# Seven block products per pair of residues for two value projections, and squares ordered ahead of copies in the attention

## Chip, cores and metric

One core of one Trainium2 chip runs one program with one launch. The metric is the device time in microseconds (us) from start to end of an execution. The page's names: PE is TensorE's matmuls, PEld its weight loads, DVE is VectorE, ACT ScalarE, POOL GpSimd, SP SyncE.

## What is computed

The program computes several transformer-like blocks for 512 tokens of width 1024, in float32. The change is in the first block, in its attention. With `h = rms_norm(x)`, the projection `proj = h @ w_in` gives queries, keys and values for three groups of eight heads of width 64:

```
qkv_a = qkv_a.reshape(b, s, 3, N_ATTN_GROUPS, HEADS_PER_GROUP, HEAD_DIM_A)
qa = rms_norm(qkv_a[:, :, 0], q_norm[i])
ka = rms_norm(qkv_a[:, :, 1], k_norm[i])
va = qkv_a[:, :, 2]
for gi, (win, dil) in enumerate(((128, 1), (512, 4), (2048, 16))):
    o_g, lse_g = dilated_window_attention(qa[:, :, gi], ka[:, :, gi], va[:, :, gi], win, dil)
mix_w = jax.nn.softmax(jnp.stack(lses, axis=0), axis=0)
```

Group 0 attends within a window of 128 tokens; groups 1 and 2 attend with a step of 4 and 16. So the kernel keeps the values of group 0 by blocks of 128 consecutive tokens, and those of the groups 1 and 2 by residue: block b holds the tokens b, b + 4, b + 8, ...

## The kernel before

Five engines run one hand-written order each, and meet at semaphores. All weights come in one stream of 1 MB fills through `ring`, four slots in SBUF. SP requests fill n + 4 once `slot_free` says that the first matmul of fill n + 1 is done (line 4348). The activations lie transposed in `hT`: eight chunks of 128 features (partitions) by 512 tokens.

**Values (lines 800 to 828).** `values_pe` goes over three groups, eight chunks k and four blocks b. The stationary operand is a block of tokens of `hT`, the moving one 512 columns of weights. For group 0 a block is 128 tokens side by side; for groups 1 and 2 it is `ap[:, b::4]`, every fourth token (`tokens_of`, line 797). The groups take two fills each, and PSUM banks 0 to 3, 4 to 7, 0 to 3. `values_dve` first makes four differences of quarters of `hT` into `in_sums` (lines 814 to 820), which the attention's projections need, then copies each group's four banks to `va` (line 824). ScalarE and POOL have nothing to do with the values, but for POOL's sums on the weights of the first projection fill (`slot_sums_pool`, lines 740 to 748).

**Projections in the attention (lines 702 to 796).** Queries and keys come from 12 fills of 28 matmuls each: seven block products instead of eight, for two tiles of 128 features and two halves of the tokens. The products' sums of weights are made by POOL in place, those of the activations are `in_sums`. The parts land in the two banks of `acc` (6 and 7). ScalarE copies the first two (`parts_out_act`, line 757, after product 1) and the third product's (`swap_out_act`, line 762, after product 3) to `kept`; VectorE joins the rest (`left_dve`, `right_dve`, `last_dve`). The last join ends with a tick (line 1051) that raises `qk_out`. Product 4 of a fill waits for the first copy, product 6 for the second.

**The loop of units (lines 934 to 955, 1012 to 1030, 1118 to 1138).** The attention proper has 32 units n: scores, maxima, exponentials, a transposition of the probabilities, the product with the values. In a unit, TensorE runs `turn_probs(n)`, `scores(n + 2)`, two to four products of the projection fills (`qk_parts`, by a fixed table of steps), then `head_sums(f)` for a fill f that became complete, and `mix_values(n)`. `head_sums` waits for the squares of that fill. ScalarE runs in a unit `turned(n)` (line 997), the first copy of the fill in work (and its second copy, if the same unit holds that), then `square(f)` of the fill that became complete (lines 968 and 970), else the second copy, `exps(n + 2)` (line 988), and `root(f)` (lines 976 and 979: logarithm and exponential, each with its table load):

```
turned(n)
for f in fills_of_step(n, "two"):
    parts_out_act(e, f)
    if f in fills_of_step(n, "left"):
        swap_out_act(e, f)
for f in done:
    square(f)
```

A fill completes in one unit and the next fill's first two products fall into the next, so the squares of the one and the copies of the other stand in the same unit (n = 0, 3, 6, 8, 11, 14, 16, 19, 22). In n = 6, 14 and 22 both copies stand there.

Later stages wait on counts of the same semaphores (`seven`, `seven_read`, `w_sum`, `base_in`, `h_sum`).

## Time and profile before

| | |
|---|---|
| median of 3 runs | 2614.75 us (2613.24 to 2618.49) |
| the profiled execution | 2618.45 us |
| its span, first to last instruction | 2616.0 us |
| TensorE's mean granted clock | 0.992 |
| TensorE matmuls busy | 2539.7 us (97%) |
| VectorE, ScalarE, POOL busy | 1303.1, 640.2, 329.5 us |
| moved by DMA | 227.41 MB, mean 87 GB/s |

A profile is one execution. Its page gives busy time by engine, the chain of work that ended last and the costliest groups; the trace behind it answers by stretch, by line and by wait. A float32 matmul stands there as two records, and so does its weight load. "Idle before" a group is the time that its engine had nothing in work, with what ended it. All of TensorE's products of this kernel have line 404, the helper that issues them, and are told apart by operands and time. The values are the stretch from 20.2 to 102.7 us, the attention follows until about 357 us.

### The profile page before, as it was taken

The page shows a single profiled execution, that of the slowest core. Times are in us where ns is not written, and L with a number is a line of the kernel's source. Part 1 is how long each engine was busy: PE and PEld are TensorE (multiplying, and loading weights), DVE is VectorE, ACT ScalarE, POOL GpSimd, SP SyncE. Part 2 cuts the span into 40 slices and gives each one's busy share as a digit, 9 for nine tenths or more (in the row PEclk, how much of TensorE's full clock was granted, in tenths as well). Part 3 has the DMA queues.
Part 4 walks back from the last instruction along what each step waited for, and adds up shares of the span by engine and source line. Part 5 has one row for each costly group of instructions (what it writes and reads, how often), then busy time and mean ns, then how long its engine had stood idle before and what let it go on. Part 6 is the DMA issues. An engine that isn't in the chain of part 4 may idle for free.

```text
span 2616.0 us, 38542 instructions
## 1 busy us (share of the span) xinstructions
PE 2539.7 (97%) x15741; PEld 1748.8 (67%) x15741; DVE 1303.1 (50%) x2873; ACT 640.2 (24%) x1168; POOL 329.5 (13%) x315
## 2 busy tenths in 40 slices
PE   8999998999999999999999999999999999999998
PEld 4766756777775684444444446688864575888887
DVE  2244565757632251000035845676765675777733
ACT  1156643323430222110011144212110122121201
POOL 0222115445441400000001000000000000000000
PEclk9999999999999999999999999999999999999999
DMA  4211111111113232444413110222223212222222
GB/s 188 77 63 49 49 56 58 39 45 52 49 50 138 88 109 81 167 171 161 174 67 113 65 48 33 89 81 97 81 97 112 97 35 81 84 94 81 95 83 80
DMA packets 32520, 227.41 MB, mean 87 GB/s; under 512 B 3552, under 2 KB 4192, under 8 KB 6112
## 3 DMA queue, kind: packets, MB, share of 16 engines
q1 hardware_dynamic: 30384, 219.50, 23.5%
q10 hardware_dynamic: 1968, 5.51, 0.6%
q8 instruction: 125, 2.05, 0.3%
q14 instruction: 43, 0.35, 0.0%
HBM read 222.90 MB, written 2.10 MB: 86 GB/s over the span
## 4 chain that ended last, share of the span: by engine, by line
PE 90%; DVE 4%; ACT 3%; issue 2%; POOL 1%; DMA 0%; ACTq 0%; DVEq 0%; POOLq 0%
PE psum L404 88%; PE psum L907 1%; DVE work L1613 0%; ACT work L970 0%; PE psum L2977 0%; PE psum L2638 0%; ACT work L3031 0%; PE psum L1262 0%; ACT work L968 0%; ACT work L976 0%; ACT L976 0%; ACT work L988 0%; DVE work L1920 0%; POOL ring L1455 0%; POOL ring L1438 0%
## 5 line engine op out<-in xcount | busy, mean ns | idle before, releaser
L404 PE MATMUL psum<-hT,ring 128*128 128x256 f32 (+2 forms) x2872 | 542.8, 370 | 4.0 <-issue 1.7
L404 PEld LDWEIGHTS psum<-hT,ring 128*128 128x128 f32 (+1 forms) x2872 | 371.9, 161 | 135.7 <-issue 94.0
L404 PE MATMUL psum<-work,ring 128*128 128x256 f32 (+1 forms) x1176 | 378.0, 472 | 4.6 <-ACT work L3903 2.4
L404 PEld LDWEIGHTS psum<-work,ring 128*128 128x128 f32 x1176 | 222.0, 190 | 144.3 <-issue 121.6
L404 PE MATMUL psum<-xT,ring 128*128 128x256 f32 (+2 forms) x1184 | 293.1, 400 | 15.6 <-POOL ring L1438 7.1
L404 PE MATMUL psum<-work,mixT 128*128 128x256 f32 (+2 forms) x1332 | 289.3, 379 | 1.2 <-DVE mixT L4118 0.7
L404 PEld LDWEIGHTS psum<-work,mixT 128*128 128x128 f32 (+1 forms) x1332 | 232.1, 182 | 47.7 <-issue 16.3
L404 PE MATMUL psum<-work 32*32 32x32 f32 (+8 forms) x5374 | 255.5, 248 | 8.4 <-issue 3.7
L404 PEld LDWEIGHTS psum<-work 32*32 32x32 f32 (+5 forms) x5374 | 210.5, 124 | 78.0 <-issue 51.9
L404 PEld LDWEIGHTS psum<-xT,ring 128*128 128x128 f32 (+1 forms) x1184 | 211.0, 188 | 71.2 <-issue 25.7
L404 PE MATMUL psum<-ring,work 128*128 (+1 forms) x568 | 247.0, 593 | 0.6 <-DVE work L3198 0.6
L404 PEld LDWEIGHTS psum<-ring,work 128*128 128x128 f32 x568 | 106.7, 190 | 131.1 <-issue 127.9
L3502 DVE SCALAR_TENSOR_TENSOR work<-work,vec 128x512 f32<-128x512 f32 x176 | 125.6, 748 | 67.3 <-ACT work L3441 67.3
L3420 POOL TENSOR_TENSOR ring<-ring,vec 128x1024 f32<-128x1024 f32 x6 | 11.3, 1898 | 1098.0 <-DMA ring<-stream_dram 1098.0
L404 PE MATMUL psum<-mixT,ring 128*128 128x512 f32 x320 | 146.7, 604 | 1.9 <-ACT mixT L3057 1.4
L3491 DVE TENSOR_TENSOR work<-work,psum 128x256 f32<-128x256 f32 x294 | 115.8, 417 | 64.2 <-PE psum L404 62.6
L404 PE MATMUL psum<-ring,hT 128*128 128x512 f32 (+1 forms) x304 | 131.7, 592 | 1.0 <-DVE ticks L379 1.0
L404 PEld LDWEIGHTS psum<-ring,hT 128*128 128x128 f32 x304 | 72.5, 240 | 56.7 <-issue 39.9
L2732 DVE SCALAR_TENSOR_TENSOR work<-psum,work 128x256 f32<-128x256 f32 x28 | 13.0, 482 | 194.3 <-ACT work L2714 193.8
L404 PEld LDWEIGHTS psum<-mixT,ring 128*128 128x128 f32 x320 | 61.0, 194 | 69.1 <-issue 64.7
L3434 ACT ACTIVATE work<-psum 128x256 f32<-128x256 f32 x42 | 16.1, 384 | 323.4 <-PE psum L404 323.4
L547 ACT ACTIVATE work<-xT 128x512 f32<-128x512 f32 x56 | 34.7, 628 | 224.6 <-DVE xT L2163 185.4
(498 smaller groups left out, 2757.1 us busy)
## 6 DMA issues: line engine op xcount, KB each, us to landing
ring<-stream_dram SPq DMA_DIRECT2D x204, 1024.0 KB, 4.8
con<-consts_dram SPq DMA_DIRECT2D x1, 2953.0 KB, 13.5
mixT<-x_dram ACTq DMA_DIRECT2D x4, 512.0 KB, 6.6
work<-x_dram ACTq DMA_DIRECT2D x4, 512.0 KB, 6.3
out_dram<-mixT SPq DMA_DIRECT2D x4, 512.0 KB, 3.6
work<-p_dram ACTq DMA_DIRECT2D x1, 512.0 KB, 6.0
con<-ssm_dram ACTq DMA_DIRECT2D x1, 512.0 KB, 3.6
vec<-vecs_dram SPq DMA_DIRECT2D x1, 378.0 KB, 5.9
```

The source lines that it names most:

```text
L404: ins = self.eng.matmul(out, lhsT, rhs, start=start, stop=stop)
L547: nc.scalar.activation(squares[:, k, :], xT[:, k, :], ACT.Square).then_inc(S["x_squares"], 1)
L907: ins = e.eng.transpose(psum[:, 2, at:at + P], a_pr[:, u.d, at:at + P], ident)
L2732: nc.vector.scalar_tensor_tensor(out=act_tok[:, s, :], in0=psum[:, gate_up_bank(ex, s), 256:512], scalar=slot_weight[:, ex, s:s + 1], in1= ...
L3420: ins = nc.gpsimd.tensor_tensor(w, w, bc(V(gain), P), ALU.mult)
L3434: nc.scalar.activation(base[:, j % 2, :], seven(j, 0), ACT.Copy).then_inc(S["base_in"], 1)
L3491: nc.vector.tensor_tensor(o, in0, in1, ALU.add).then_inc(S["seven_read"], 1)
L3502: nc.vector.scalar_tensor_tensor(out=y, in0=fpad[:, half, t - 1:t - 1 + T], scalar=wv[:, t - 1:t], in1=y, op0=ALU.mult, op1=ALU.add).then_ ...
```

## The change

For the groups 1 and 2 the blocks are taken in pairs: two residues (0 and 1, then 2 and 3) by two halves of the 1024 features, times two halves of the features by two halves of the 512 columns, with seven products of 128 tokens by 256 columns over four chunks each, in place of eight. Four such pairs (two groups, two pairs of residues) are numbered j = 0 to 3. VectorE first makes four differences of `hT` by residue (`residue_sums`, into `mixT`), then four sums on the weights of a group's two fills in eight steps (`value_weights_dve`, one of them in place in `ring`), then the four old differences, the copies of group 0, join 0, the weights of group 2, joins 1 to 3. ScalarE copies one bank for each pair (`values_act`). Group 0 is as before. The two fills of a group are both held until both pairs have used them: the second slot is given free at product 4 of the second pair. TensorE's wait ahead of the attention is now for the joins of the first three pairs.

In the attention `square(f)` of the done fills stands directly behind `turned(n)`, ahead of the copies of the next fill.

Elsewhere in the kernel the counts waited for grow by the four products' sets (`PAIRED` = 4 and `IN_SUMS` = 8 in place of 0 and 4), with no other change.

```
                 if i == 1:
                     if f == 0:
-                        e.eng.wait_ge(S["h_sum"], 4)
+                        e.eng.wait_ge(S["h_sum"], IN_SUMS)
...
+        residue_sums = mixT[:, 4:12, :].rearrange("p a t -> p (a t)").rearrange("p (n k c t) -> p n k c t", n=4, k=4, c=2)
+        value_sums = work[:, GROUPS * NB * 512:GROUPS * NB * 512 + 12 * T].rearrange("p (g n k t) -> p g n k t", g=2, n=3, k=4)
+        value_base, value_two = kept[:, T:T + T // 2], kept[:, T + T // 2:2 * T]
+        PAIRED, RESIDUE_SUMS, IN_SUMS = 4, {"one": 1, "three": 2, "two": 3, "four": 4}, 8
+        VALUE_SUMS = {"one": 2, "three": 4, "two": 6, "four": 8}
+        def value_part(j, i):
+            n, at = ((0, 0), (0, 1), (1, 0), (2, 0), (2, 1), (1, 1), (3, 0))[i]
+            return psum[:, 4 - 4 * (j % 2) + n, T // 2 * at:T // 2 * at + T // 2]
         def values_pe(e):
-            for g in range(GROUPS):
-                for k in range(DC):
-                    if k % 4 == 0:
-                        e.eng.wait_ge(S[e.landing()], e.landed())
-                        w = e.slot(ring)
-                    for b in range(NB):
-                        if g == 2 and k == 0 and b == 0:
-                            e.eng.wait_ge(S["values_out"], 1)
-                        ins = e.mm(psum[:, 4 * (g % 2) + b, :], tokens_of(g, b, hT[:, k, :]), w[:, 512 * (k % 4):512 * (k % 4) + 512],
-                                   k == 0, k == DC - 1)
-                ins.then_inc(S["values"], 1)
+            for k in range(DC):
+                if k % 4 == 0:
+                    e.eng.wait_ge(S[e.landing()], e.landed())
+                    w = e.slot(ring)
+                for b in range(NB):
+                    ins = e.mm(psum[:, b, :], tokens_of(0, b, hT[:, k, :]), w[:, 512 * (k % 4):512 * (k % 4) + 512],
+                               k == 0, k == DC - 1)
+            ins.then_inc(S["values"], 1)
+            fill_at["values"] = e.c["fill"].n
+            for j in range(PAIRED):
+                g, pair = divmod(j, 2)
+                f = fill_at["values"] + 2 * g
+                if pair == 0:
+                    e.eng.wait_ge(S[e.landing()], e.landed())
+                    low = e.slot(ring)
+                high = ring[:, (f + 1) % RING, :]
+                def block(w, half):
+                    return [w[:, 512 * k + 256 * half:512 * k + 256 * half + 256] for k in range(4)]
+                def tokens(k0, r):
+                    return [hT[:, k0 + k, 2 * pair + r::4] for k in range(4)]
+                def product(i, tok, weights):
+                    for k in range(4):
+                        ins = e.mm(value_part(j, i), tok[k], weights[k], k == 0 and i in (0, 2, 3, 6), k == 3 and i in (1, 4, 5, 6))
+                    ins.then_inc(S["seven"], 1)
+                t1, t2, t3, t4 = ([residue_sums[:, n, k, pair, :] for k in range(4)] for n in range(4))
+                s1, s2, s4 = ([value_sums[:, g, n, k, :] for k in range(4)] for n in range(3))
+                if j == 1:
+                    e.eng.wait_ge(S["values_out"], 1)
+                if j >= 2:
+                    e.eng.wait_ge(S["base_in"], j - 1)
+                product(0, tokens(0, 0), block(low, 0))
+                e.eng.wait_ge(S["w_sum"], 8 * g + VALUE_SUMS["one"])
+                e.eng.wait_ge(S["h_sum"], RESIDUE_SUMS["one"])
+                product(1, t1, s1)
+                e.eng.wait_ge(S["loaded%d" % ((f + 1) % RING)], 16 * ((f + 1) // RING + 1))
+                if j >= 2:
+                    e.eng.wait_ge(S["seven_read"], 7 * (j - 1))
+                product(2, tokens(4, 0), block(high, 0))
+                e.eng.wait_ge(S["w_sum"], 8 * g + VALUE_SUMS["three"])
+                e.eng.wait_ge(S["h_sum"], RESIDUE_SUMS["three"])
+                product(3, t3, block(low, 1))
+                if pair == 1:
+                    e.slot(ring)
+                e.eng.wait_ge(S["w_sum"], 8 * g + VALUE_SUMS["two"])
+                e.eng.wait_ge(S["h_sum"], RESIDUE_SUMS["two"])
+                product(4, t2, s2)
+                e.eng.wait_ge(S["w_sum"], 8 * g + VALUE_SUMS["four"])
+                product(5, tokens(4, 1), s4)
+                e.eng.wait_ge(S["h_sum"], RESIDUE_SUMS["four"])
+                product(6, t4, block(high, 1))
+            e.c["fast"].n += PAIRED
+        def values_act(e):
+            for j in range(PAIRED):
+                e.eng.wait_ge(S["seven"], 7 * j + 2)
+                if j >= 1:
+                    e.eng.wait_ge(S["seven_read"], 7 * (j - 1) + 6)
+                nc.scalar.activation(kept[:, 0:T], psum[:, 4 - 4 * (j % 2), :], ACT.Copy).then_inc(S["base_in"], 1)
+            e.c["fast"].n += PAIRED
+        def value_weights_dve(e, g):
+            f = fill_at["values"] + 2 * g
+            (a11, a21), (a12, a22) = ([ring[:, n % RING, :].rearrange("p (k h t) -> p h k t", k=4, h=2)[:, h, :, :] for h in range(2)]
+                                      for n in (f, f + 1))
+            s1, s2, s4 = (value_sums[:, g, n, :, :] for n in range(3))
+            for n in (f, f + 1):
+                e.eng.wait_ge(S["loaded%d" % (n % RING)], 16 * (n // RING + 1))
+            for step, (o, in0, in1, op) in enumerate(((s1, a21, a22, ALU.add), (a21, a11, a21, ALU.subtract),
+                                                      (s2, s1, a11, ALU.subtract), (s4, a12, s2, ALU.subtract))):
+                if step:
+                    e.eng.wait_ge(S["w_sum"], 8 * g + 2 * (1, 1, 3)[step - 1])
+                for k in (slice(0, 2), slice(2, 4)):
+                    nc.vector.tensor_tensor(o[:, k, :], in0[:, k, :], in1[:, k, :], op).then_inc(S["w_sum"], 1)
+        def value_joins_dve(e, j):
+            g, pair = divmod(j, 2)
+            read = S["seven_read"]
+            x, y = va[:, 1 + g, 2 * pair, :], va[:, 1 + g, 2 * pair + 1, :]
+            first, second = slice(0, 256), slice(256, 512)
+            zero, one = kept[:, 0:T // 2], kept[:, T // 2:T]
+            e.eng.wait_ge(S["base_in"], j + 1)
+            e.eng.wait_ge(S["seven"], 7 * j + 5)
+            nc.vector.tensor_tensor(value_base, zero, value_part(j, 4), ALU.add).then_inc(read, 1)
+            e.eng.wait_ge(read, 7 * j + 1)
+            nc.vector.tensor_tensor(value_two, value_base, value_part(j, 3), ALU.add).then_inc(read, 1)
+            e.eng.wait_ge(read, 7 * j + 2)
+            nc.vector.tensor_tensor(y[:, second], value_two, one, ALU.add).then_inc(read, 1)
+            e.eng.wait_ge(read, 7 * j + 3)
+            nc.vector.tensor_tensor(one, value_base, one, ALU.add).then_inc(read, 1)
+            e.eng.wait_ge(S["seven"], 7 * j + 6)
+            nc.vector.tensor_tensor(x[:, first], zero, value_part(j, 2), ALU.add).then_inc(read, 1)
+            e.eng.wait_ge(read, 7 * j + 4)
+            nc.vector.tensor_tensor(y[:, first], one, value_part(j, 5), ALU.add).then_inc(read, 1)
+            e.eng.wait_ge(S["seven"], 7 * j + 7)
+            nc.vector.tensor_tensor(x[:, second], value_two, value_part(j, 6), ALU.add).then_inc(read, 1)
 
         def values_dve(e):
+            low, high = (hT[:, k, :].rearrange("p k (m r) -> p k r m", r=NB) for k in (slice(0, 4), slice(4, 8)))
+            xs, ys_ = slice(0, 4, 2), slice(1, 4, 2)
+            for n, (o, in0, in1) in enumerate(((0, low[:, :, ys_, :], low[:, :, xs, :]), (2, high[:, :, ys_, :], low[:, :, ys_, :]),
+                                               (1, high[:, :, ys_, :], residue_sums[:, 0, :, :, :]),
+                                               (3, high[:, :, xs, :], residue_sums[:, 1, :, :, :]))):
+                if n >= 2:
+                    e.eng.wait_ge(S["h_sum"], (1, 3)[n - 2])
+                nc.vector.tensor_tensor(residue_sums[:, o, :, :, :], in0, in1, ALU.subtract).then_inc(S["h_sum"], 1)
+            value_weights_dve(e, 0)
             k1, k2, early, late = slice(0, 4), slice(4, 8), slice(0, T // 2), slice(T // 2, T)
             for n, (o, in0, in1) in enumerate(((0, hT[:, k1, late], hT[:, k1, early]), (2, hT[:, k2, late], hT[:, k1, late]),
                                                (1, hT[:, k2, late], in_sums[:, 0, :, :]),
                                                (3, hT[:, k2, early], in_sums[:, 1, :, :]))):
                 if n >= 2:
-                    e.eng.wait_ge(S["h_sum"], (1, 3)[n - 2])
+                    e.eng.wait_ge(S["h_sum"], RESIDUE_SUMS["four"] + (1, 3)[n - 2])
                 nc.vector.tensor_tensor(in_sums[:, o, :, :], in0, in1, ALU.subtract).then_inc(S["h_sum"], 1)
-            for g in range(GROUPS):
-                e.eng.wait_ge(S["values"], e.c["values"].next())
-                for b in range(NB):
-                    ins = nc.vector.tensor_copy(va[:, g, b, :], psum[:, 4 * (g % 2) + b, :])
-                    if b < NB - 1:
-                        ins.then_inc(S["dve_chain"], 1)
-                        e.eng.wait_ge(S["dve_chain"], e.c["dve_chain"].next())
-                ins.then_inc(S["values_out"], 1)
+            e.eng.wait_ge(S["values"], e.c["values"].next())
+            for b in range(NB):
+                ins = nc.vector.tensor_copy(va[:, 0, b, :], psum[:, b, :])
+                if b < NB - 1:
+                    ins.then_inc(S["dve_chain"], 1)
+                    e.eng.wait_ge(S["dve_chain"], e.c["dve_chain"].next())
+            ins.then_inc(S["values_out"], 1)
+            value_joins_dve(e, 0)
+            value_weights_dve(e, 1)
+            for j in range(1, PAIRED):
+                value_joins_dve(e, j)
+            e.c["fast"].n += PAIRED
 
...
             for n in range(UNITS_A):
                 done = [AHEAD // 2 - 1] if n == 0 else fills_of_step(n - 1, "last")
                 turned(n)
+                for f in done:
+                    square(f)
                 for f in fills_of_step(n, "two"):
                     parts_out_act(e, f)
                     if f in fills_of_step(n, "left"):
                         swap_out_act(e, f)
-                for f in done:
-                    square(f)
                 for f in fills_of_step(n, "left"):
                     if f not in fills_of_step(n, "two"):
                         swap_out_act(e, f)
...
             e.c["stage"].next()
-            e.eng.wait_ge(S["values_out"], 2)
+            e.eng.wait_ge(S["seven_read"], 7 * (PAIRED - 1))
             e.mark("attn")
...
             e.eng.wait_ge(S["stage"], e.c["stage"].next())
             e.mark("values")
+            values_act(e)
             e.eng.wait_ge(S["stage"], e.c["stage"].next())
```

## Rows read from the trace of the kernel before

**Rows 1.** Parts 1 and 4 of the page: busy time, and the chain that ended last

```profile
PE 2539.7 (97%) x15741; PEld 1748.8 (67%) x15741; DVE 1303.1 (50%) x2873; ACT 640.2 (24%) x1168; POOL 329.5 (13%) x315
...
PE 90%; DVE 4%; ACT 3%; issue 2%; POOL 1%; DMA 0%; ACTq 0%; DVEq 0%; POOLq 0%
```

**Rows 2.** Busy us (instructions) of PE, PEld, DVE, ACT, POOL; clock; DMA: values, attention

```profile
20.20:102.70 82.50, 82.47 (x192) 51.73 (x193) 10.25 (x12) 0.00 (x0) 2.53 (x2) 1.00 0.28 106
102.70:330.00 227.30, 211.09 (x1190) 160.23 (x1189) 109.74 (x406) 122.50 (x231) 58.22 (x46) 0.98 0.16 56
```

**Rows 3.** Waits of TensorE, 99 to 350 us: total us, times, longest

```profile
PE psum L404 <- ACT work L970: 11.5, 9, 2.3
```

**Rows 4.** Busy time as in rows 2, within group 0 and within group 1

```profile
20.30:47.20 26.90, 26.90 (x63) 12.00 (x64) 4.63 (x4) 0.00 (x0) 0.00 (x0) 1.00 0.40 161
...
58.00:85.50 27.50, 27.50 (x65) 19.74 (x64) 2.76 (x4) 0.00 (x0) 2.53 (x2) 1.00 0.21 76
```

**Rows 5.** Timeline of TensorE's weight loads, attention: start us, us taken

```profile
107.70 3.43 PEld L404 LDWEIGHTS psum<-xT,ring 128*128 128x128 f32 x16
```

**Rows 6.** Timeline of TensorE's weight loads under single-column matmuls, near 972 us

```profile
971.70 1.86 PEld L404 LDWEIGHTS psum<-con,work 128*128 128x128 f32 x16 [0.20 <-DVE work L555]
```

**Rows 7.** Page part 6; groups by line, 0 to 200 us; timelines of VectorE and SP

```profile
con<-consts_dram SPq DMA_DIRECT2D x1, 2953.0 KB, 13.5
...
L820 DVE TENSOR_TENSOR xT<-hT 128x1024 f32<-128x1024 f32 x2 | 2.4, 1221 | 0.0
...
11.26 1.23 SPq L610 DMA_DIRECT2D ring<-stream_dram  x2
...
113.63 0.41 DVE L777 TENSOR_TENSOR work<-mixT,psum 128x256 f32<-128x256 f32 x1
...
126.94 0.60 DVE L777 TENSOR_TENSOR work<-mixT,psum 128x256 f32<-128x256 f32 x1
```

**Rows 8.** Timeline of the unit n = 3 and the next, 168 to 183 us

```profile
168.80 0.06 DVE L1051 MEMSET ticks<- 128x1 f32 x1
...
168.91 0.60 ACT L997 ACTIVATE work<-psum 128x512 f32<-128x512 f32 x1 [2.69 <-PE psum L907]
...
173.21 0.60 ACT L757 ACTIVATE mixT<-psum 128x512 f32<-128x512 f32 x1 [3.70 <-PE psum L404]
...
174.35 1.27 ACT L970 ACTIVATE work<-work 64x512 f32<-64x512 f32 x2
...
175.67 1.09 PE L404 MATMUL psum<-work,con 64*64 64x512 f32 x8 [0.77 <-ACT work L970]
...
176.75 1.28 ACT L976 ACT_TABLE_LOAD   x1
...
181.43 0.58 ACT L997 ACTIVATE work<-psum 128x512 f32<-128x512 f32 x1
...
182.15 0.66 PE L404 MATMUL psum<-work 128*64 128x128 f32 x8
```

**Rows 9.** Timeline of the unit n = 6, 189 to 199 us

```profile
189.90 0.06 DVE L1051 MEMSET ticks<- 128x1 f32 x1 [0.50 <-DVE work L791]
...
192.98 0.60 ACT L757 ACTIVATE mixT<-psum 128x512 f32<-128x512 f32 x1 [3.48 <-PE psum L404]
...
198.68 1.09 PE L404 MATMUL psum<-work,con 64*64 64x512 f32 x8 [2.28 <-ACT work L970]
```

**Rows 10.** As rows 2, clock 0.50; timeline of TensorE, n = 6, n = 14

```profile
200.20:203.40 3.20, 3.20 (x14) 1.93 (x11) 0.96 (x6) 3.16 (x4) 0.00 (x0) 0.50 0.02 5
...
199.70 0.77 PE L404 MATMUL psum<-work 128*64 128x128 f32 x8
...
202.60 2.43 PE L404 MATMUL psum<-xT,ring 128*128 128x256 f32 x8
...
260.17 0.66 PE L404 MATMUL psum<-work 128*64 128x128 f32 x8
...
261.98 1.99 PE L404 MATMUL psum<-xT,ring 128*128 128x256 f32 x8
```

More of the change, by code:

```diff
@@ L2130, in out_weights_dve @@
             if n >= 2:
-                e.eng.wait_ge(S["seven"], 7 * (n - 2) + 6)
+                e.eng.wait_ge(S["seven"], 7 * (PAIRED + n - 2) + 6)
             nc.vector.tensor_tensor(s1, a21, a22, ALU.add).then_inc(S["w_sum"], 1)
-            e.eng.wait_ge(S["w_sum"], 4 * n + 1)
+            e.eng.wait_ge(S["w_sum"], 4 * (PAIRED + n) + 1)
             nc.vector.tensor_tensor(a21, a11, a21, ALU.subtract).then_inc(S["w_sum"], 1)
             nc.vector.tensor_tensor(s2, s1, a11, ALU.subtract).then_inc(S["w_sum"], 1)
-            e.eng.wait_ge(S["w_sum"], 4 * n + 3)
+            e.eng.wait_ge(S["w_sum"], 4 * (PAIRED + n) + 3)
             nc.vector.tensor_tensor(s4, a12, s2, ALU.subtract).then_inc(S["w_sum"], 1)
@@ L2211, in x_added @@
         def x_added(c):
-            return 7 * (c // 2) + 6 + c % 2
+            return 7 * (PAIRED + c // 2) + 6 + c % 2
         def x_turn_chunk_pe(e, c):
@@ L2301, in out_kept_act @@
         def out_kept_act(e, n):
-            e.eng.wait_ge(S["seven"], 7 * n + 2)
+            e.eng.wait_ge(S["seven"], 7 * (PAIRED + n) + 2)
             if n == 0:
@@ L3269, in program @@
                      work[:, FC * T:FC * T + 4 * T]]
-        DOWN_AT, G_AT = 2 * FAST + NB, 12
+        DOWN_AT, G_AT = 2 * FAST + NB + PAIRED, IN_SUMS + 8
         def group(q, i):
```

40 lines of the change are left out of this document (20 added, 20 removed).

## The prediction

> **What bounds the kernel now.** I read the page first [rows 1]: TensorE is busy 97% of the span and carries 90% of the chain that ended last, while VectorE has 4% and ScalarE 3% of it. DMA is nowhere on the chain. So a microsecond taken from TensorE's queue early on is a microsecond of the end, unless another engine becomes late. The table by stage [rows 2] then gives the two stages that are edited: the values (20.2 to 102.7 us) have TensorE busy without a hole, 82.47 of 82.50 us in 192 records, and only 10.25 us of VectorE and none of ScalarE; the attention (102.7 to 330 us) has 16.2 us in which TensorE is not busy. The waits of TensorE in the attention [rows 3] name the largest part of these holes: 11.5 us in nine places until the squares of line 970 are done, at most 2.3 us at a time. The profiled execution took 2618.45 us (span 2616.0); the median of the three runs is 2614.75, 3.7 us less. I make the sum of differences against the profiled one and apply it to the median, which I forecast. No change means within 0.2%, 5.2 us.
>
> **Part 1, the values of two groups.** Removed: 2 x 8 x 4 = 64 products of 512 columns. In the trace each product is two matmul records (96 products, 192 records [rows 2]), 0.430 us each, so the 64 cost 128 x 0.430 = 55.0 us. Added: 4 pairs x 7 products x 4 chunks = 112 products of 256 columns, 224 records. The attention's products have this form. Sixteen of its weight loads, one to a matmul record, take 3.43 us, the last of them 0.19 [rows 5]: one starts every (3.43 - 0.19) / 15 = 0.216 us. At that price the new work is 224 x 0.216 = 48.3 us, a gain of 6.7.
>
> That price holds for weights that lie side by side. Products 0, 2 and 5 take the tokens straight from hT with a step of four (12 of the 28 in each pair, 96 records), the other four from the packed differences. The kernel before loads with that step in its groups 1 and 2: a load there takes 19.74 us / 64 = 0.308 us, in group 0, without the step, 12.00 / 64 = 0.19 us [rows 4]. Under 0.43 us of matmul the longer load is hidden; under 0.216 us it isn't, if it counts in full. What it counts is bounded so. Below: all hidden, gain 6.7 us. Above: loads follow one another as those of rows 5 do, 0.19 us plus a gap of 0.025; the stepped ones would come each 0.333 us, 96 x 0.117 = 11.2 us dearer, a loss of 4.5. The nearest row says which: under matmuls of a single column, sixteen loads of 0.19 us take 1.86 us [rows 6], so one starts each (1.86 - 0.19) / 15 = 0.111 us: 0.08 us of a load's record overlaps the next load. So I take 0.308 - 0.08 = 0.228 us for a stepped one, 0.012 over the matmul, 96 x 0.012 = 1.2 us. **Part 1: -5.5 us.**
>
> The Trainium skill (SBUF — State Buffer, "Door 1: The DMA port swizzle") has a rule that speaks against this: lines of 16 bytes, each access that crosses into a new one paying a penalty. By it every token of these loads pays, as the 0.308 against 0.19 us bears out; it has no figure for a load, and so moves nothing in the sum.
>
> What stands beside: TensorE's first 32 products stay (27.5 us, until 47.7). VectorE in that time makes four subtractions of 1024 elements with a step. Without one they took 1.22 us [rows 7]; a stepped operand took 0.60 where 256 elements otherwise took 0.42 [rows 7], so up to 2 us each, 8 in all. Then the weights' sums, 8 x 512 elements, 0.7 us each (half of 1.22, rounded up), 5.6 us, behind the landing of the third and fourth slot, issued at 11.3 to 12.5 us [rows 7]; at the 13.5 us of the slowest issue on the page that is 26 us. Then the four old subtractions, 4.9 us. End near 26 + 5.6 + 4.9 = 37 to 40 us, 8 us before the copies of group 0. I cost all this at nothing; were the cover gone, product 1 at 49.6 us would wait. The joins: ScalarE copies one bank (0.6 us), VectorE adds seven times 256 elements, 7 x 0.42 to 0.60 = 3 to 4 us for 12.2 us of TensorE. The second weights' sums (5.6 us) stand behind join 0 (near 61 us) and are wanted near 74. Behind the last product one addition of 0.42 us is left, and TensorE goes on anyway, since it waits for join 2 alone; ScalarE is wanted first at the end of the attention's second product, 16 x 0.216 = 3.5 us in. SP's fills: the first attention fill is now requested at product 4 of the second pair, near 67 us, and used near 97, with two sums of POOL between; even 13.5 us of transfer leave room. The third is requested at product 4 of the last pair, near 92, and used 24 us later. Nothing waits.
>
> **Part 2, squares first.** In nine of the units of the loop (n = 0, 3, 6, 8, 11, 14, 16, 19, 22) ScalarE squares a finished fill and copies the next one's parts in one unit. Rows 8 show one: turned(3) is done at 169.5, the fill's tick came at 168.80, and ScalarE is then idle 3.70 us until product 1 of the next fill has ended; only behind that copy come the squares, the last of them until 175.62. TensorE has ended its third product at 174.90 and waits 0.77 us with the head sums. With the squares first they run 169.5 to 171.4, 1.8 us before the copy can start; exps(n+2) behind them come 1.9 us earlier. Six units are like this, 6 x 0.77 = 4.6 us. In n = 6, 14, 22 both copies come first, and the wait is 2.28 us [rows 9]: 6.8 us. The tick there comes at 189.90, the squares would end by 191.9, and the copy starts at 192.98 as before. In n = 0 the fill's last joins are late on VectorE, so the copy may start up to 1.9 us later than now; product 4, which needs it, comes two products and the whole of a unit's small ones later, over 4 us. That sums to the 11.5 us of rows 3.
>
> What is late next: mix(n+1) on TensorE needs turned(n+1), which stands behind the root of the head sums (a table load, a logarithm, a table load, an exponential): in rows 8 from 176.75 until 182.01, 5.3 us from the end of the head sums (176.76), against 5.4 us until TensorE begins mix(n+1) at 182.15. That is tight, but the first table load now falls before the head sums end, as ScalarE is done with exps(n+2) 1.9 us sooner. I take nothing for it.
>
> The clock: behind two of the three long waits the granted clock is 0.50 (1.2 of 2.4 GHz) for 3.4 us [rows 10]. The same work then takes from 199.70 to 205.03, 5.33 us, instead of from 260.17 to 263.97, 3.80: 1.53 us more. The third long wait was followed by none. With the waits gone I take both back: 3.1 us (bounds 0 and 3.1 plus one more such stretch elsewhere). **Part 2: -14.6 us.**
>
> **Sum:** -5.5 - 14.6 = -20.1 us: 2598.4 against the profiled execution, 2614.75 - 20.1 = 2594.7 for the median.
>
> **Rivals.** *Stepped loads count in full* (0.333 us): part 1 is +4.5, the sum -10.1, 2604.7. For it: rows 5 show loads with a gap between them. Against: rows 6. Chance 0.12. *The root is late next*: the table load doesn't move ahead, and TensorE waits up to 1.28 us in each of the nine units before mix(n+1), 11.5 us: 2606.2. For: the margin is 0.1 us. Against: ScalarE is done with exps(n+2) 1.9 us sooner, more than a table load. Chance 0.12. *The squares don't come earlier*, because the tick they wait for is late on VectorE (the change doesn't do what it says): 2609.3, at the edge of no change. Against: the ticks at 168.80 and 189.90 [rows 8, 9]. Chance 0.06. *Slower:* a stepped load doesn't run beside the matmul before it, so that each of the 96 records costs 0.308 + 0.213 us, 0.305 over the 0.216: +29.3 - 6.7 - 14.6 = +8.0, 2622.8. It decides from a spacing of 0.49 us on. Against: in groups 1 and 2 of the kernel before stepped loads left the matmuls at 0.43 us. Chance 0.04.
>
> The Trainium skill (TensorE: Matmul & The Clock Gate, "The mechanism") says loads overlap running matmuls only when their row groups differ; here all use all rows, which would be this last rival. The 0.19 us loads within 0.216 us of rows 5 disagree.
>
> **Numbers.** The forecast has 0.66. The range goes down to 2614.75 - 6.7 - 14.6 - 3.1 (two further slow stretches gone) = 2590, 2589 with rounding, and up over the first rival and most of the second, 2606. Faster by over 0.2%: 0.66 + 0.12 + 0.12 = 0.90; within: 0.06; slower: 0.04.
>
> **What would show it.** The attention's first 256-wide product from ring and hT at 97.2 us instead of 102.73; records with stepped loads 0.23 us apart; no wait for line 970's squares but those of the old prologue and end; squares straight behind the copy of line 997; granted clock 1.00 near the head sums of fills 4 and 10; a span of 2596. It is wrong if TensorE waits in the values for a join or a weights' sum, or if a wait for line 997 takes the place of the squares.

## The result, and the profile after

The changed kernel took 2602.45 us (median of 7, 2599.51 to 2609.24), the kernel before 2615.66 us beside it (median of 7, 2613.24 to 2621.03). The ratio is 0.9945 (95% interval 0.9935 to 0.9954): 14.4 us, or 0.55%, faster. The forecast was 20.1 us and 2594.7; 2602.45 lies inside the range of 2589 to 2606, in its upper half. The profiled execution took 2601.21 us (span 2599.3), against 2618.45 (2616.0) before.

The head and lines of parts 1, 3 and 4 of the page of the changed kernel, to be read against [rows 1]:

```profile
span 2599.3 us, 38802 instructions
PE 2530.7 (97%) x15837; PEld 1755.3 (68%) x15837; DVE 1330.7 (51%) x2913; ACT 642.8 (25%) x1172; POOL 328.6 (13%) x315
...
q8 instruction: 126, 2.06, 0.3%
...
PE 91%; DVE 4%; ACT 2%; issue 2%; POOL 1%; DMA 0%; ACTq 0%; DVEq 0%; POOLq 0%
```

TensorE's busy time fell by 9.0 us and the span by 16.7. TensorE has 96 records more, VectorE 40 more.

**The values.** TensorE's timeline of the changed kernel at the first pair, and VectorE's up to the copies of group 0 (start us, us taken, engine, line, operation):

```profile
49.53 1.89 PE L404 MATMUL psum<-work,mixT 128*128 128x256 f32 x8
51.25 2.03 PE L404 MATMUL psum<-ring,hT 128*128 128x256 f32 x8
53.12 1.89 PE L404 MATMUL psum<-ring,mixT 128*128 128x256 f32 x8
...
97.65 1.89 PE L404 MATMUL psum<-hT,ring 128*128 128x256 f32 x8
...
38.01 1.23 DVE L930 TENSOR_TENSOR xT<-hT,xT 128x1024 f32<-128x1024 f32 x1
47.88 2.14 DVE L933 COPY work<-psum 128x512 f32<-128x512 f32 x3 [8.65 <-PE psum L404]
```

A product whose tokens lie side by side is followed by the next after 51.25 - 49.53 = 1.72 us, 0.215 us a record; one with the step of four after 53.12 - 51.25 = 1.87 us, 0.234 a record. The forecast had 0.216 and 0.228. The attention's first product from hT and ring starts at 97.65 us where it stood at 102.73: 5.1 us. The timeline has no hole: VectorE was idle for 8.65 us before the copies, so all its new work lay under group 0, as the forecast had it (8 us to spare).

**The attention.** The waits of TensorE, 99 to 330 us, to be read against [rows 3]:

```profile
PE psum L404 <- ACT mixT L757: 2.7, 1, 2.7
PE psum L404 <- ACT work L1111: 1.8, 1, 1.8
PE psum L404 <- DVE work L777: 1.5, 1, 1.5
PE psum L404 <- DVE ticks L1165: 1.3, 1, 1.3
```

The 11.5 us behind the squares (line 970, now 1084) are gone from the list. The three waits above the last row are of the prologue and the end, and were there before at the same lengths. The last one was 0.3 us. The timeline of the unit n = 3 shows the new order that [rows 8] lacked:

```profile
162.94 0.06 DVE L1165 MEMSET ticks<- 128x1 f32 x1
...
164.19 1.27 ACT L1084 ACTIVATE work<-work 64x512 f32<-64x512 f32 x2
...
167.35 0.60 ACT L757 ACTIVATE mixT<-psum 128x512 f32<-128x512 f32 x1 [1.89 <-PE psum L404]
...
168.97 1.09 PE L404 MATMUL psum<-work,con 64*64 64x512 f32 x8
169.08 1.28 ACT L1090 ACT_TABLE_LOAD   x1
```

The squares are done at 165.46, 1.89 us before the copy; the head sums (168.97) follow without a wait, and the first table load starts while they still run.

**Where it was given back.** I took the start of the same TensorE instruction in both traces, all the way down. The changed kernel is ahead by 5.1 us at the attention's start, by 20.5 us at 325 us, and by 20.6 us near 2080 us. That looks like the forecast, but part of it is slow clock stretches that fell in one trace and not in the other: with each trace's stretches of granted clock 0.50 counted at half their length, the lead is 17.1 us at 325 us and 15.5 near 2080. At the end it is 16.8 as read and 11.6 so counted. The mean granted clock was 0.994 in this execution and 0.992 in the one before, which alone is some 0.002 x 2600 = 5 us (2 to 8 with the rounding), so the pair of profiles flatters the change. The loss behind 2080 us is in two steps. TensorE's timeline of the changed kernel there:

```profile
2063.57 5.40 PE L404 MATMUL psum<-hT,ring 128*32 128x128 f32 x170 [0.42 <-DVE hT L576]
2070.58 2.49 PE L404 MATMUL psum<-hT,ring 128*32 128x128 f32 x83 [1.60 <-issue]
...
2076.63 7.20 PE L404 MATMUL psum<-hT,ring 128*32 128x128 f32 x256
...
2090.64 4.86 PE L404 MATMUL psum<-hT,ring 128*32 128x128 f32 x169
2097.56 2.50 PE L404 MATMUL psum<-hT,ring 128*32 128x128 f32 x84 [2.06 <-issue]
...
2106.30 7.17 PE L404 MATMUL psum<-hT,ring 128*32 128x128 f32 x256
```

and of the kernel before:

```profile
2084.17 7.79 PE L404 MATMUL psum<-hT,ring 128*32 128x128 f32 x256 [0.42 <-DVE hT L576]
2095.61 7.20 PE L404 MATMUL psum<-hT,ring 128*32 128x128 f32 x256
...
2109.62 7.17 PE L404 MATMUL psum<-hT,ring 128*32 128x128 f32 x256
...
2123.06 7.17 PE L404 MATMUL psum<-hT,ring 128*32 128x128 f32 x256
```

The first set of 256 products starts 20.6 us earlier after the change, the second 19.0, the fourth 16.8. In the first and the third TensorE stops in the middle of 256 identical products, after the 170th and the 169th, for 1.60 and 2.06 us. "issue" says that it waited for nothing that the profile shows: no semaphore, no other engine. This stage is 1700 us behind the last edited line. The experiments had to find out what these stops are, and whether the change causes them.

### The profile page after: what moved, and what is told of

Its sections match the earlier page's. It is cut to its first block, busy times and chain, and to the rows that moved or that the text cites. A ratio compares the mean times of both kernels' runs of the same rounds, so it can differ in the third digit from the quotient of the medians.

```text
span 2599.3 us, 38802 instructions
## 1 busy us (share of the span) xinstructions
PE 2530.7 (97%) x15837; PEld 1755.3 (68%) x15837; DVE 1330.7 (51%) x2913; ACT 642.8 (25%) x1172; POOL 328.6 (13%) x315
## 3 DMA queue, kind: packets, MB, share of 16 engines
q8 instruction: 126, 2.06, 0.3%
## 4 chain that ended last, share of the span: by engine, by line
PE 91%; DVE 4%; ACT 2%; issue 2%; POOL 1%; DMA 0%; ACTq 0%; DVEq 0%; POOLq 0%
PE psum L404 89%; PE psum L1021 1%; DVE work L1727 0%; PE psum L3091 0%; PE psum L1376 0%; DVE work L2034 0%; PE psum L2752 0%; ACT work L3145 0%; DVE work L1724 0%; POOL ring L1569 0%; POOL ring L1552 0%; DMA mixT<-x_dram 0%; ACT work L617 0%; DVE work L2010 0%; POOL work L1585 0%
## 5 line engine op out<-in xcount | busy, mean ns | idle before, releaser
L404 PE MATMUL psum<-work,mixT 128*128 128x256 f32 (+2 forms) x1396 | 304.4, 379 | 1.2 <-DVE mixT L4232 0.7
L404 PEld LDWEIGHTS psum<-work,mixT 128*128 128x128 f32 (+1 forms) x1396 | 244.3, 183 | 49.2 <-issue 16.4
L404 PE MATMUL psum<-ring,hT 128*128 (+2 forms) x240 | 92.8, 540 | 1.0 <-DVE ticks L379 1.0
L404 PE MATMUL psum<-hT,mixT 128*128 128x256 f32 x336 | 79.4, 379 | 0.0
```

Source lines behind the costliest of these rows:

```text
L404: ins = self.eng.matmul(out, lhsT, rhs, start=start, stop=stop)
```

## The experiments

An execution's loss to the clock scatters by several microseconds. So beside the ratio I give the **clock-free time**: each execution's time multiplied by its mean granted clock, which takes off what was lost at the lower level, averaged over the runs. (Every execution also ends in 8.8 us or more of the lower level behind its last matmul, which costs nothing. The product takes off about 4.4 us for it, in every kernel nearly alike, so the differences stand.) For the kernel before that is 2597.0 us (44 runs beside the experiments, standard error 0.3), for the changed one 2584.7 (18 runs, 0.4): 12.3 us less. The mean loss itself is 19.6 us before (2616.6 x 0.0075) and 19.1 us after.

**Each part alone.** `only_values` puts line 970's squares back behind the copies and keeps the seven products:

```diff
                 turned(n)
-                for f in done:
-                    square(f)
                 for f in fills_of_step(n, "two"):
                     parts_out_act(e, f)
...
+                for f in done:
+                    square(f)
```

> The seven block products alone, squares behind the copies as before. My theory (each of the 96 records with stepped weights costs 0.233 us, all others 0.216, nothing waits): the first product of the attention at 97.6 us, TensorE's waits for the squares again 11.5 us in nine places, and the whole 5.1 us (0.20%) faster than the kernel before, with some us of scatter from the clock's slow stretches. Rival (part 1 costs code, so that TensorE stops more often for instructions later on): a gain of 5.1 by 102 us of which 2 to 4 us are gone at the end.

2617.28 us, ratio 1.0002 (0.9993 to 1.0011). By alignment it is 5.4 us ahead at the attention's start, 5.5 at 300 us, 12.2 at 1700 to 2000 us (slow clock stretches that fell elsewhere are in that), and only 7.0 from 2200 us on. Its timeline has the stops at the same products, after the 170th of the first 256 and the 169th of the third:

```profile
2072.00 5.40 PE L404 MATMUL psum<-hT,ring 128*32 128x128 f32 x170 [0.42 <-DVE hT L576]
2078.43 2.49 PE L404 MATMUL psum<-hT,ring 128*32 128x128 f32 x83 [1.03 <-issue]
...
2105.68 4.16 PE L404 MATMUL psum<-hT,ring 128*32 128x128 f32 x84 [2.24 <-issue]
```

Its clock-free time is 2595.4 us (12 runs, error 0.4), 1.3 below the kernel before beside it (2596.7, 17 runs, error 0.4). So part 1 gains its 5 us in the values and gives most of it back near 2080 and 2106 us.

`only_squares` makes the opposite move in the kernel before: the two lines of the squares go ahead of the copies, the values keep their eight products.

> The order of the squares alone, values as before. My theory: 11.5 us of waits gone from the attention and about 3 us of half clock with them, 14.6 us (0.56%) up to 325 us of the trace; then 1.0 us given back at the last fill's tick (a wait of 1.3 in place of 0.3 us). Rival (the loss behind 325 us comes with any earlier start of the later stages, not with the code of part 1): the same 2 to 5 us are lost behind 350 us here too.

2601.67 us, ratio 0.9951 (0.9938 to 0.9964); clock-free 2585.8, 10.9 us below the kernel before beside it (2596.7). All nine waits for the squares are gone, no stop stands near 2070 to 2110 us, and the tick's wait grew from 0.3 us to the same 1.3:

```profile
PE psum L404 <- DVE ticks L1051: 1.3, 1, 1.3
```

Part 2 alone does nearly what both parts together do (10.9 of 12.3 us clock-free). And an earlier start of the later stages doesn't bring the stops: here they start as early and there is none.

**Is it the kernel or the execution?** `after_again` and `before_again` are the two kernels once more, unedited.

> The changed kernel once more. If TensorE's stops for instructions belong to places in the code, its stops near 442, 2069 and 2095 us (1.85, 1.6 and 2.1 us) come again within 1 us of these times; if they are chance, they come elsewhere or not at all. The clock's slow stretches I expect at other places than in the first profile in part. Time 0.9945 of before.

> The kernel before, once more, for its trace. If stops for instructions belong to the code, they are again near 455 and 546 us and none near 2069 or 2095; if they are chance, the number changes. Span 2612 to 2618 us.

`after_again`: 2602.32 us, ratio 0.9953 (0.9939 to 0.9967), its stops at 2070.53 (2.04 us) and 2097.79 (2.24). `before_again`: 2617.43 us, no stop in that stage. The stops belong to the kernel. The slow clock stretches are less fixed. The kernel before had them at 138.7, 200.1, 319.6, 394.7 and 548.3 us in one execution, and at 137.4, 198.8, 260.3, 372.9 and 410.5 in the other, where some lasted 6.8 us instead of 3.4. The two of the changed kernel agree nearly, but a third (`after_third`, below) has its own at 133.0 (6.8 us), 320.7 and 354.8 (6.8 us).

**Is it where the code lies?** The page's queue q8 moves the instructions: 126 packets and 2.06 MB, so 16 KB each (125 packets and 2.05 MB before). Part 1 gives TensorE 192 instructions for the 96 records (a load and a matmul each) and 14 waits more: 206. Every block behind the values then ends 206 instructions earlier in the work. If a stop is a block that arrives late, filling up with idle instructions must move it. `after_pad50` adds 50 of them (100 satisfied waits, of which two share one instruction: the page counts 38852 instructions instead of 38802), so that with the 206 a block is full again. Its length is an estimate from the page: 2 x 15837 records of TensorE in 126 blocks are 251 a block, and some waits come on top, so I took 256:

```diff
             e.eng.wait_ge(S["ident_in"], 16)
+            for _ in range(100):
+                e.eng.wait_ge(S["ident_in"], 16)
             for b in range(NB):
```

> The changed kernel with 50 instructions more on TensorE (waits that are long fulfilled) while it is idle ahead of its first product. The change added 206 instructions to its code, of which 256 go into one block of code that is loaded; with 50 more the blocks end at the same instructions as in the kernel before. My theory (a block that falls due while SP's 1 MB fill is on the way comes late, and where blocks end decides which fall due then): no stop of TensorE for instructions near 2070 and 2097 us, and 3.5 to 5 us less than the changed kernel, 0.993 of the kernel before. Rival (the stops come from the later stages starting earlier): the stops stay, 0.9945.

> The kernel before with 206 instructions more on TensorE in its idle time ahead of the first product, nothing else. My theory: it gets the stops that the change brought, 1.0 to 2.2 us each near 2085 and 2112 us of its trace, and is 3 to 5 us (0.1 to 0.2%) slower than the kernel before, if the extra instructions themselves fit into the idle time (else by what the first product starts later). Rival: same time as before, no such stops.

`after_pad50`: 2600.47 us, ratio 0.9945 (0.9930 to 0.9959), no better than the changed kernel's. By the ratio alone this is inconclusive. The stops themselves are gone from TensorE's timeline:

```profile
2069.37 7.82 PE L404 MATMUL psum<-hT,ring 128*32 128x128 f32 x256 [0.42 <-DVE hT L576]
...
2080.82 7.19 PE L404 MATMUL psum<-hT,ring 128*32 128x128 f32 x256
...
2094.84 7.17 PE L404 MATMUL psum<-hT,ring 128*32 128x128 f32 x256
```

`before_pad206` has 412 such waits (206 instructions) in the kernel before. It brings the stops into a kernel that has neither part of the change, at the same products (83 and 84 follow the stop, as in the changed kernel). TensorE's timeline, its first product and the stage:

```profile
27.24 3.50 PE L640 MATMUL psum<-con,work 128*128 128x128 f32 x16 [27.24 <-issue]
...
2104.88 2.49 PE L404 MATMUL psum<-hT,ring 128*32 128x128 f32 x83 [0.69 <-issue]
...
2132.11 4.10 PE L404 MATMUL psum<-hT,ring 128*32 128x128 f32 x84 [2.06 <-issue]
```

It took 2637.6 us, ratio 1.0090 (1.0075 to 1.0106). But most of that is the padding: its instructions run from 4.8 to 27.1 us of the trace, and TensorE's first product moved from 10.6 to 27.24 us. It is 15.3 us behind the kernel before at 102 us, 14.6 at 2000, and 19.5 after 2200, a step of 4.9 us in that stage, of which 1.7 are a slow stretch at 2132.8 us. Over its six runs the clock-free time is 19.0 us above that of the kernel before beside it; less the 15.3 of the start that leaves 3.7.

The traces hold a sharper test of the blocks. Number TensorE's instructions in order (loads, matmuls and waits). All 80 stops for "issue" of 0.5 us or more that the 14 traces show behind TensorE's first product then stand at a number 193 or 194 above a multiple of 256. The two in this stage have the numbers 25025 and 26561, 6 x 256 apart, in the changed kernel, in `only_values` and in `before_pad206` alike. So a block is 256 instructions, and stops happen at its ends. They don't happen at each: the changed kernel's trace has 7 of them in 126 blocks.

To settle the size, both versions ran again on one chip:

> The changed kernel beside the padded one on one chip, to weigh the stops for instructions in time and not in traces alone. My theory: median 4 us above that of the padded kernel run with it, and the same after the loss by the clock (time multiplied by one less the granted clock) is taken off each run, 2584 to 2586 us against 2580 to 2581. Rival (what the stops cost comes back as slow stretches of the clock in the padded kernel): medians equal within 2 us, the granted clock lower in the padded kernel.

> The padded changed kernel beside the unpadded one. My theory: no stops near 2070 and 2097 us again, 0.9930 of the kernel before. Rival: 0.9945 as the unpadded one, with a granted clock 0.001 lower.

2602.86 us (ratio 0.9951, 0.9937 to 0.9964) against 2598.47 (0.9937, 0.9923 to 0.9950): 4.4 us. Over all runs the padded kernel is at 2580.7 us clock-free (11 runs, error 0.4) against 2584.7: **4.0 us for the place of the block ends**. The 50 instructions themselves cost 0.1 us at most: they run in idle time, and the first product starts at 10.69 instead of 10.61 us. In the stage near 2100 us alone, counted by alignment without the slow stretches, the three traces of the changed kernel lose 3.9, 4.8 and 3.4 us against the kernel before, the two padded ones 0.2 and 0.0. TensorE's waits for "issue" behind 345 us go the same way, but by less: 5.4 us in the kernel before, 9.0 in the changed one, 6.7 with the padding, whose other stops, before 700 us, are longer in this pair.

```profile
PE psum L404 <- issue: 9.0, 9, 2.1
...
PE psum L404 <- issue: 6.7, 8, 1.9
```

**What a stepped load costs.** In `packed` ScalarE, idle until the values' joins, copies the stepped tokens of products 0, 2 and 5 side by side into free columns of `work` during group 0:

```diff
                 def tokens(k0, r):
-                    return [hT[:, k0 + k, 2 * pair + r::4] for k in range(4)]
+                    return [packed[:, {(0, 0): 0, (4, 0): 1, (4, 1): 2}[k0, r], k, pair, :] for k in range(4)]
...
+            for n, src in enumerate((low[:, :, xs, :], high[:, :, xs, :], high[:, :, ys_, :])):
+                for c in range(2):
+                    ins = nc.scalar.activation(packed[:, n, :, c, :], src[:, :, c, :], ACT.Copy)
+                ins.then_inc(S["packed"], 1)
```

> The changed kernel with the tokens of products 0, 2 and 5 copied side by side by ScalarE first (six copies in the first 28 us), so that no weight load has a step. My theory: those products take 1.725 instead of 1.865 us each, the attention's first product starts 1.7 us earlier, near 96.0 us, nothing waits. Whether the end follows depends on the code blocks as in the changed kernel: 0.9940 of the kernel before, or the same as the changed kernel. Rival (the step isn't what makes the loads long): start near 97.6 us as before.

The products now come 1.73 us apart throughout, and the attention's first product starts at 95.51 us, by alignment 2.1 us earlier than in the changed kernel (the whole queue is 0.5 us early already at 19.6 us, ahead of the values, so 1.6 us are the loads', as expected):

```profile
47.16 1.89 PE L404 MATMUL psum<-ring,work 128*128 128x256 f32 x8
48.89 1.89 PE L404 MATMUL psum<-work,mixT 128*128 128x256 f32 x8
...
95.51 1.89 PE L404 MATMUL psum<-hT,ring 128*128 128x256 f32 x8
```

The time, 2604.95 us, ratio 0.9954 (0.9938 to 0.9970), does not show it; clock-free it is 2582.9, 1.8 us below the changed kernel. The profiled execution had a granted clock of 0.989.

A first form of the next experiment, `narrow`, left half of each product out and gave no result. `split` makes each product of 256 columns two of 128, under which a load can't hide:

```diff
-                        ins = e.mm(value_part(j, i), tok[k], weights[k], k == 0 and i in (0, 2, 3, 6), k == 3 and i in (1, 4, 5, 6))
+                        for h in range(2):
+                            c = slice(128 * h, 128 * h + 128)
+                            ins = e.mm(value_part(j, i)[:, c], tok[k], weights[k][:, c], k == 0 and h == 0 and i in (0, 2, 3, 6),
+                                       k == 3 and h == 1 and i in (1, 4, 5, 6))
```

> The changed kernel with each block product of the values cut into two of 128 columns, each with its own load of the same weights, nothing left out: 448 records of 0.107 us of matmul in place of 224 of 0.213. So the loads bound them. My theory (a load repeats after its record less 0.08 us): 0.23 us a record where the weights have a step (3.7 us for the 16 records of a product), 0.112 us where they lie side by side (1.8 us). Rival (a stepped load keeps the next one out for its whole 0.308 us): 4.9 us a product. Rival 2 (the 0.233 us of the changed kernel are a matmul slowed by its load, not a bound of loads): under 0.2 us a record, under 3.2 us a product.

One execution, 2621.8 us against a median of 2617.95 for the kernel before. Sixteen records each:

```profile
51.45 1.95 PE L404 MATMUL psum<-work,mixT 128*128 128x128 f32 x16
53.23 3.89 PE L404 MATMUL psum<-ring,hT 128*128 128x128 f32 x16
56.97 1.95 PE L404 MATMUL psum<-ring,mixT 128*128 128x128 f32 x16
```

Side by side, (53.23 - 51.45) / 16 = 0.111 us; stepped, (56.97 - 53.23) / 16 = 0.234 us, the same as under 256 columns. So 0.234 us is the load's own rate: its record of 0.308 [rows 4] less 0.074, as 0.111 is 0.19 less 0.08 [rows 6].

**What is left in the attention.** `early_pad` is the padded kernel with ScalarE's copy of fill 2 ahead of the first two exponentials of the prologue, which removes the wait for line 757 of 2.7 us:

```diff
             square(1)
+            parts_out_act(e, 2)
             exps(0)
             exps(1)
-            parts_out_act(e, 2)
```

> The changed kernel with the 50 instructions of padding and, in the prologue of the attention, ScalarE's first copy of fill 2 ahead of the exponentials of the units 0 and 1 instead of behind them. My theory: TensorE's wait of 2.7 us for line 757 goes, the head sums of fill 1 come earlier, and fill 3 starts 2 to 3.6 us earlier; 0.9935 of the kernel before. Rival (the chain through the root of fill 1 and VectorE's joins sets the start of fill 3): the wait moves to line 777 and nothing is won. On the clock: if every removed wait took its slow stretch along, the mean granted clock would rise above 0.993; I now expect it to stay at 0.992 to 0.993.

2594.73 us, ratio 0.9907 (0.9890 to 0.9924), more than was expected; clock-free 2578.1 (4 runs, error 0.7), 2.6 us below the padded kernel. The next fill's first product starts at 141.06 instead of 144.69 us, and the wait that follows the removed one grew from 1.5 to 2.2 us (its line is 779 here, 777 without the padding):

```profile
141.06 2.84 PE L404 MATMUL psum<-hT,ring 128*128 128x256 f32 x8 [2.21 <-DVE work L779]
```

`best` puts together the packed tokens, the early copy and 49 instructions of padding. In the units with both copies it also moves `exps(n + 2)` ahead of the second one, so that the last root isn't late:

```diff
                 for f in fills_of_step(n, "two"):
                     parts_out_act(e, f)
-                    if f in fills_of_step(n, "left"):
-                        swap_out_act(e, f)
+                both = fills_of_step(n, "two") == fills_of_step(n, "left") != []
+                if both:
+                    exps(n + 2)
                 for f in fills_of_step(n, "left"):
-                    if f not in fills_of_step(n, "two"):
-                        swap_out_act(e, f)
-                if n + 2 < UNITS_A:
+                    swap_out_act(e, f)
+                if n + 2 < UNITS_A and not both:
                     exps(n + 2)
```

> All together: changed kernel, padding to the old ends of the code blocks, packed tokens by ScalarE, the early copy of fill 2, and in the three units with two copies the exponentials ahead of the second copy, so that the root comes 0.9 us earlier. My theory: the attention's first product at 96 us; wait for the last fill's tick at most 0.5 in place of 1.3 us; no stops near 2070 and 2097 us; 0.9920 to 0.9930 of the kernel before. Rival (gains before 400 us are lost in the stages that follow): 0.9945 as the changed kernel.

2591.83 us, ratio 0.9895 (0.9879 to 0.9912): faster than both kernels, and by more than was expected. Clock-free it is 2575.7 us (4 runs, error 0.6), 20.4 below the kernel before beside it; the other 5.5 of the 25.9 us between their means are clock. By alignment it is 6.7 us ahead of the kernel before at 102 us, 21.9 at 300 and 23.1 at the end. The tick's wait is down to 0.4 us:

```profile
PE psum L404 <- DVE ticks L1176: 0.4, 1, 0.4
```

## Why the prediction was right, and what it missed

The sign and both mechanisms held, in the places forecast. The sum was 20.1 us, the ratio says 14.4. The range covers that by luck: its upper part was there for stepped loads in full and for a late root, and what filled it is a cost that the prediction doesn't name. Point by point, without the clock:

- **Part 1 in the values: -5.5 forecast, -5.1 measured.** The spacing of side-by-side records was right. The stepped one came at 0.234 us instead of 0.228: 96 x (0.234 - 0.216) = 1.7 us instead of 1.2, which is the whole difference. `split` confirms the reading of [rows 6]: a load's record overlaps the next one by its last 0.07 to 0.08 us, stepped or not.
- **Part 2, the nine waits: -11.5 forecast, and none is left.** The squares stand ahead of the copy in each unit, with 1.89 us to spare in n = 3.
- **"What is late next": the root, costed at nothing.** It was right in eight units of nine. In the last fill TensorE's wait for the tick grew from 0.3 to 1.3 us. The timeline of the changed kernel there:

```profile
300.56 1.28 ACT L1090 ACT_TABLE_LOAD   x1
...
305.37 0.75 DVE L1170 SCALAR_TENSOR_TENSOR work<-work,vec 128x512 f32<-128x512 f32 x1 [1.71 <-ACT work L1093]
...
310.19 0.06 DVE L1165 MEMSET ticks<- 128x1 f32 x1
310.30 1.98 PE L404 MATMUL psum<-hT,ring 128*128 128x512 f32 x4 [1.29 <-DVE ticks L1165]
```

  The head sums end at 300.24, but the table load starts only at 300.56, behind the second copy and the exponentials. The root is done at 305.3 and VectorE's chain behind it ends in the tick. This is the mechanism of the second rival, at another consumer and at one place: 1.0 us instead of 11.5. In `best`, where the exponentials go first, 0.9 us of it is gone.
- **The clock: -3.1 forecast, about zero measured.** This step failed. The stretches near 200 and 319 us did go with the waits: the head sums of fill 4 run at granted clock 1.00 now. But others came at 353 and 377 us, where the kernel before had clock 1.00. The windows of the changed kernel and then of the kernel before (columns as in [rows 2], the clock third from the end):

```profile
353.40:356.60 3.20, 3.20 (x8) 2.57 (x9) 2.99 (x5) 1.70 (x2) 0.00 (x0) 0.50 0.29 61
```

```profile
353.40:356.60 3.20, 3.20 (x24) 1.66 (x20) 0.98 (x4) 2.22 (x4) 0.00 (x0) 1.00 0.02 5
```

  Over 44 and 18 runs the mean loss went from 19.6 to 19.1 us (errors 0.6 and 0.9). The lower bound of that term in the prediction, 0, was the right value to take. It isn't so in every kernel: `early_pad` and `best` lose 16.5 us (8 runs, error 1.0) where the kernel before beside them loses 21.7 (7 runs, 1.5), and `only_squares` 17.2 (1.6) against 20.5 (0.9). With so few runs that is a hint of a gain, and no run shows what makes the difference.
- **The term that was missing: +4.0 us for code.** The prediction counted what the new instructions do and not that they lengthen TensorE's program. They shift the ends of all later 16 KB blocks, and two of these now fall where the next block isn't there in time, in a stage where TensorE goes through a block in 3.5 us. Shown four ways: the stops vanish with 50 idle instructions more, they appear in the kernel before with 206 more, they stand at block ends in every trace, and on one chip the padding is worth 4.4 us. It takes most of what part 1 gained: -5.1 + 4.0 = -1.1 us, where `only_values` has -1.3 clock-free.

The sum with the measured terms: -5.1 - 11.5 + 1.0 + 4.0 = -11.6 us, against 12.3 clock-free and 14.4 by the ratio. The clock adds 0.5 us on the mean of all runs, 12.8 in all; the rest is within what the ratios scatter (the three of the unedited changed kernel give 14.4, 12.3 and 12.8 us).

Of the rivals, *stepped loads count in full* would have had spacings of 0.333 us, and *slower* of 0.52; measured 0.234. The Trainium skill (TensorE: Matmul & The Clock Gate, "The mechanism") says in one line that a load overlaps a running matmul only where their row groups differ, and in another that TensorE also pulls a load ahead when it goes to the background weight buffer. The prediction took up the first alone; this kernel's trace, with 0.19 us loads of all rows inside records 0.215 us apart, disagrees with that line and fits the other. *The squares don't come earlier* fell with the tick at 162.94 and the squares at 164.19.

Why these two blocks come late and others not is in part open. The DMA records of the traces show the next block start to load once TensorE passes a block's end, and how soon depends on SP's 1 MB fills. In the changed kernel TensorE passes ends at 2064.7 and 2091.7 us, fills stream from 2065.1 and from 2092.1 us on, and the blocks start to load only at 2068.2 and 2095.1, 3.5 and 3.4 us later. In the padded kernel (`pad50_again`) the ends are passed at 2064.4 and 2089.8 us, 1.1 and 1.2 us ahead of their fills, and the blocks start to load 0.8 and 0.3 us later. All 14 traces agree at these two places. In the seven with stops the end is passed within 0.6 us of the fill's start, and the block starts to load 2.8 to 3.9 us later. In the seven without, it is passed 1.1 or 1.2 us ahead of the fill, and the block starts to load 0.2 to 1.2 us later. No run moved the fills alone, so that they are the cause isn't shown. Open too is what sets the place of a slow clock stretch.

## What to carry to other kernels

A change that adds some hundred instructions to the busiest engine can cost microseconds far behind itself (here 206, and 4.0 us). Compare "issue" stops of the two traces over the whole span, and when a stage that nobody edited loses time, pad the program by a few dozen idle instructions before blaming the change. Don't book a gain from the clock for removed waits unless the granted clock has been averaged over many runs. Follow a squeezed engine's order to the last unit of a loop, too, where fewer products stand between the late result and its user.

## What the runs showed of the hardware that was not expected

- TensorE's stops for its own code: 0.7 to 2.2 us each, in the middle of 256 identical products, with no semaphore in play. They stand at the ends of blocks of 256 instructions (16 KB). Whether this kernel has them in the stage near 2100 us goes with what is added ahead of it: 206, 207 (`packed`) and 654 instructions (`split`, 142 over two blocks) bring two, 0 and 256 none.
- Satisfied waits are not free: 206 instructions with two satisfied waits each ran from 4.78 to 27.14 us, 0.11 us an instruction, and delayed TensorE's first product by 16.7 us. The 50 of `after_pad50` ran in idle time and delayed it by 0.1.
- A weight load with a step of four is a record of 0.308 us and repeats every 0.234; side by side 0.19 and 0.111. Under matmuls of 256 columns (0.216 us) the stepped one is just too long, by 0.018 us; the four products in seven with packed tokens are spaced as if their loads cost nothing (0.215).
- The clock's slow stretches moved rather than went: 11.5 us of idle time taken out of the attention left the mean loss at 19.1 of 19.6 us. In the two fastest kernels it was lower, 16.5 against 21.7 beside them, on 8 and 7 runs.
